# MLP down projections by rows: activations stationary, weights moving, and the last norm by rows

## What is computed

```python
D_MODEL, D_FF, SEQ = 1024, 4096, 512
...
h = _rmsnorm(x, mlp_norm_g)          # x: [512, 1024]
u = jnp.square(jax.nn.relu(h @ w_up))   # [512, 4096]
x = x + u @ w_down
return _rmsnorm(x, final_norm_g)
```

## Time and profile before

| what | value |
|---|---|
| median of 3 runs | 1023.85 us (1023.57 to 1024.23) |
| the profiled execution | 1023.27 us |
| its span, first to last instruction | 1021.5 us |
| PE busy | 1012.0 us (99%) |
| DVE, ACT, POOL busy | 52%, 42%, 57% |
| DMA share of 16 engines (queue q1) | 29.2% |
| granted TensorE clock, mean | 0.999 |

### The profile page before, as it was taken

One profiled execution on the slowest core, in us unless ns is written; L12 is line 12 of the kernel. 1 busy time (PEld: TensorE's weight loads), 2 busy tenths in 40 slices (PEclk: granted clock), 3 DMA queues, 4 the chain that ended last, 5 costly groups with the idle time before them and its releaser, 6 DMA issues.

```text
span 1021.5 us, 12838 instructions
## 1 busy us (share of the span) xinstructions
PE 1012.0 (99%) x5063; PEld 857.5 (84%) x5063; DVE 527.4 (52%) x895; ACT 425.0 (42%) x687; POOL 582.3 (57%) x724
## 2 busy tenths in 40 slices
PE   9999999999999999999999999999999999999997
PEld 8888888888888888888899977888888888888887
DVE  5781356775366843445679997846123113212323
ACT  4653455556534524443346685533223212222332
POOL 4555556556565774565557877447545545545441
PEclk9999999999999999999999999999999999999999
DMA  6322222122352125323123123222322322322312
GB/s 230 128 83 85 85 81 83 42 83 83 115 174 83 48 76 188 124 83 118 52 79 124 43 83 114 92 84 83 123 84 83 123 83 83 124 83 83 121 45 83
DMA packets 93788, 98.63 MB, mean 97 GB/s; under 512 B 3314, under 2 KB 88848, under 8 KB 93728
## 3 DMA queue, kind: packets, MB, share of 16 engines
q1 hardware_dynamic: 93728, 97.81, 29.2%
HBM read 95.71 MB, written 2.10 MB: 96 GB/s over the span
## 4 chain that ended last, share of the span: by engine, by line
PE 92%; DVE 6%; ACT 1%; issue 1%; DVEq 0%
PE ps L383 82%; PE ps L771 1%; PE ps L1803 1%; PE ps L271 1%; PE ps L803 1%; PE ps L724 1%; PE ps L722 1%; PE ps L428 1%; PE ps L503 1%; DVE ps L1286 0%; DVE tmp L1352 0%; DVE Fm L1243 0%; PE ps L932 0%; DVE Hl L1324 0%; DVE Al L1711 0%
## 5 line engine op out<-in xcount | busy, mean ns | idle before, releaser
L296 POOL TENSOR_TENSOR wlo<-raw,whi 128x256 fp32r<-128x256 f32 x664 | 515.5, 808 | 339.0 <-ACT whi L291 339.0
L383 PE MATMUL ps<-Hh,whi 128*128 128x512 f32 x816 | 321.0, 393 | 1.6 <-DVE Hl L1324 1.2
L383 PE MATMUL ps<-Hl,whi 128*128 128x512 f32 x816 | 318.0, 390 | 0.0
L291 ACT ACTIVATE whi<-raw 128x1024 fp32r<-128x1024 f32 x166 | 175.2, 1055 | 158.9 <-PE ps L383 151.0
L383 PE MATMUL ps<-Hh,wlo 128*128 128x512 f32 x816 | 205.1, 389 | 0.3 <-POOL wlo L296 0.3
L383 PE MATMUL ps<-Ah,whi 128*128 128x512 f32 (+1 forms) x576 | 196.4, 364 | 0.2 <-DVE Al L1711 0.2
L383 PE MATMUL ps<-Al,whi 128*128 128x512 f32 (+1 forms) x576 | 194.7, 361 | 0.0
L383 PEld LDWEIGHTS ps<-Hh,whi 128*128 128x128 f32 x816 | 153.3, 188 | 33.8 <-DVE Hl L1324 1.9
L383 PEld LDWEIGHTS ps<-Hh,wlo 128*128 128x128 f32 x816 | 153.1, 188 | 32.5 <-POOL wlo L296 0.7
L383 PEld LDWEIGHTS ps<-Hl,whi 128*128 128x128 f32 x816 | 153.3, 188 | 30.8
L383 PE MATMUL ps<-Ah,wlo 128*128 128x512 f32 (+1 forms) x576 | 124.5, 360 | 0.0
(11 more groups left out here) (324 smaller groups left out, 1013.7 us busy)
## 6 DMA issues: line engine op xcount, KB each, us to landing
raw<-in_w_in SPq DMA_DIRECT2D x33, 1024.0 KB, 5.1
raw<-in_w_up SPq DMA_DIRECT2D x16, 1024.0 KB, 5.4
raw<-in_w_down SPq DMA_DIRECT2D x16, 1024.0 KB, 5.1
raw<-in_w_att_out SPq DMA_DIRECT2D x4, 1024.0 KB, 5.1
raw<-in_w_sg_out SPq DMA_DIRECT2D x4, 1024.0 KB, 5.2
raw<-in_w_o SPq DMA_DIRECT2D x4, 1024.0 KB, 5.1
raw<-in_w_in SPq DMA_DIRECT2D x6, 512.0 KB, 3.7
Fm<-in_x SPq DMA_DIRECT2D x2, 1024.0 KB, 6.7
```

Of the source, the lines that this page charges most:

```text
L291: eh = A(lambda e, s=s, src=src, kk=kk: e.activation(wtile(whi, s, kk), src, ACT.Copy), raw_ev[b], used)
L296: el = G(lambda e, s=s, src=src, kk=kk, cut=cut: e.tensor_tensor(wtile(wlo, s, kk)[:, *cut], src[:, *cut], f(wtile(whi, s, kk))[:, *cut], ...
L383: return e.matmul(ps[:, bk, 0:c1 - c0], wt, x[:, k, c0:c1], start=st, stop=sp)
```

## The change

The down weights come in half-megabyte blocks of one tile: 256 rows by 512 columns. A down pass takes one half of the output columns (512) for all 512 tokens: four banks, one per 128 tokens; the stationary operand is a 128x128 block of activations, the moving one 512 columns of weights, and each weight tile serves four banks. The sums are added on DVE to a residual held by rows, `OT`, which is made once: `residual_turns`, a background generator during part 0, transposes the residual's eight tiles through banks 7 and 6. The up products of parts 1 to 3 rotate over all eight banks. The gains of the last norm are loaded once, copied to all partitions. The last 512 columns of part 3 are not a pass: their four weight tiles are kept whole in `Ah`/`Al` (free after the last up product), and each block of 128 tokens runs its 24 matmuls, then its add, square with a running sum (ACT, `accum_out`), factor, scaling and store, while the next block multiplies. The square sums by matmul, the transposes and the halves at the end are gone.

```diff
         for i in range(4):
             cols("w_up_2", 0, 1024 * i, 4)
-            cols("w_down_2", 1024 * i, 0, 4)
...
+            for h in range(2):
+                for k in range(4):
+                    cols("w_down_2", 1024 * i + 256 * k, 512 * h, 1, 2, 1)
+        n_kept = len(tiles) - 4
+
+
+        kept = [tuple(a[:, 1024 * i:1024 * i + 1024].rearrange("p (k n) -> p k n", k=2) for a in (Ah, Al))
+                for i in range(4)]
...
+                kk = blocks[b][3]
...
-                used = w_used[j - NW] if j >= NW else None
...
+                if j < n_kept:
+                    th, tl = wtile(whi, j % NW, kk), wtile(wlo, j % NW, kk)
+                    used = w_used[j - NW] if j >= NW else None
+                else:
+                    (th, tl), used = kept[j - n_kept], got["up"]
+                eh = A(lambda e, th=th, src=src: e.activation(th, src, ACT.Copy), raw_ev[b], used)
...
-                    el = G(lambda e, s=s, src=src, kk=kk, cut=cut: e.tensor_tensor(
-                        wtile(wlo, s, kk)[:, *cut], src[:, *cut], f(wtile(whi, s, kk))[:, *cut], ALU.subtract),
-                        eh, signal=(part == 3))
+                    el = G(lambda e, th=th, tl=tl, src=src, cut=cut: e.tensor_tensor(
+                        tl[:, *cut], src[:, *cut], f(th)[:, *cut], ALU.subtract), eh, signal=(part == 3))
...
-        OT = F1.rearrange("p k n -> p (k n)").rearrange("p (t c) -> p t c", t=4)
-        ot_ev = []
+        OT, Z = (F.rearrange("p k n -> p (k n)").rearrange("p (t c) -> p t c", t=4) for F in (F1, F2))
+        ot_ev = [[], []]
...
-        def turn(n, ev):
...
+        def residual_turns():
+            yield
+            yield
+            for i, n in enumerate(late_k):
+                bk = 7 - i % 2
+                for t_ in range(4):
+                    et = T(lambda e, t_=t_, n=n, bk=bk: e.transpose(
+                        ps[:, bk, 128 * t_:128 * t_ + 128], F3[:, n, 128 * t_:128 * t_ + 128], ident[:]),
+                           hm_ev[n], bank_free[bk], signal=(t_ == 3))
+                bank_free[bk] = A(lambda e, n=n, bk=bk: e.activation(
+                    OT[:, :, 128 * n:128 * n + 128], ps[:, bk, :].rearrange("p (t c) -> p t c", t=4), ACT.Copy),
+                    et, hm_ev[3])
+                ot_ev[n // 4].append(bank_free[bk])
+                if i < 7:
+                    yield
+
+        def four_banks():
+            bks = sorted(range(8), key=lambda bk: bank_age[bk])[:4]
+            taken(*bks)
+            return bks
+
+        def down_mm(bk, t_, k, w, x, start, stop, signal):
+            return T(lambda e: e.matmul(ps[:, bk, :], x[:, k, 128 * t_:128 * t_ + 128], w, start=start, stop=stop),
+                     signal=signal)
+
+        def down_pass(ahead=(3, 3, 3, 3)):
+
+            bks = four_banks()
+            q.wait("pe", *[bank_free[bk] for bk in bks])
...
+                j = at[0]
+                at[0] += 1
+                feed(j + ahead[i])
+                q.wait("pe", hi_ev[j])
+                wh, wl = wtile(whi, j % NW, 2), wtile(wlo, j % NW, 2)
+                ks = (2 * i, 2 * i + 1)
+                order = [(k, wh, x) for k in ks for x in (Hh, Hl)] + [(k, wl, Hh) for k in ks]
+                for n, (k, w, x) in enumerate(order):
+                    q.wait("pe", *acts[k], lo_ev[j] if w is wl else None)
+                    evs = [down_mm(bks[t_], t_, k, w[:, k % 2], x, i == 0 and n == 0, i == 3 and n == 5, n == 5)
+                           for t_ in range(4)]
+                w_used.append(evs[3])
+                tick()
+            return bks, evs
+
+        def down_add(h, t_, bk, em):
+            y = OT[:, t_, 512 * h:512 * h + 512]
+            e_ot[t_, h] = bank_free[bk] = V(lambda e: e.tensor_tensor(y, ps[:, bk, :], y, ALU.add), em, *ot_ev[h],
+                                            e_ot.get((t_, h)))
...
+        e_ot = {}
         bgs.append(mlp_factors())
+        bgs.append(residual_turns())
         for part in range(4):
             acts = []
-            nb = 6 if part < 3 else 4
             waiting = []
             for n in range(8):
...
+                waiting.append(single(A8h, A8l, u3ev, late_k, nb=8 if part else 6))
 
...
+            got["up"] = w_used[-1]
+            if part == 0:
+                while bgs:
+                    finish(bgs[0])
+                gl = P[:, 0:1024]
+                e_gl = q.dma("sp", gl, t["final_norm_g_2"].rearrange("(a n) -> a n", a=1).broadcast_to([128, 1024]),
+                             dsem("d_gl"), got["ss"])
+            for h in range(2 if part < 3 else 1):
+                bks, evs = down_pass((3, 3, 3, 3) if part < 3 else (3, 5, 6, 5))
+                for t_ in range(4):
+                    down_add(h, t_, bks[t_], evs[t_])
+            e_down = evs[3]
+
+
+
...
+        R4, ssq, v4 = sm[:, 180:184], sm[:, 146:154], sm[:, 154:162]
         d_out = dsem("d_out")
...
+        def squares(h, t_):
+            y, z = (a[:, t_, 512 * h:512 * h + 512] for a in (OT, Z))
+            c = 2 * t_ + h
+            ea = A(lambda e: e.activation(F4[:, c], y, ACT.Square,
+                                          accum_out=ssq[:, c:c + 1]), e_ot[t_, h], got["ss"], hm_ev[3])
+            ez = V(lambda e: e.tensor_tensor(z, y, gl[:, 512 * h:512 * h + 512], ALU.mult), e_ot[t_, h], e_gl)
+            return ea, ez
+
+        first_half = {}
+        for t_ in range(4):
+            ea, ez = squares(0, t_)
+            e0 = V(lambda e, t_=t_: e.tensor_scalar(v4[:, t_:t_ + 1], ssq[:, 2 * t_:2 * t_ + 1], 1.0 / D, EPS, ALU.mult,
+                                                    ALU.add), ea)
+            first_half[t_] = (ez, e0)
+        js = range(at[0], at[0] + 4)
+        at[0] += 4
+        bks = four_banks()
+        for t_ in range(4):
+            order = [(k, 0, x) for k in range(8) for x in (Hh, Hl)] + [(k, 1, Hh) for k in range(8)]
+            q.wait("pe", bank_free[bks[t_]])
+            for n, (k, part, x) in enumerate(order):
+                q.wait("pe", (lo_ev if part else hi_ev)[js[k // 2]])
+                em = down_mm(bks[t_], t_, k, kept[k // 2][part][:, k % 2], x, n == 0, n == 23, n == 23)
+            down_add(1, t_, bks[t_], em)
+            ea, ez1 = squares(1, t_)
+            ez0, e0 = first_half[t_]
+            r = R4[:, t_:t_ + 1]
+            e1 = V(lambda e, t_=t_: e.scalar_tensor_tensor(
+                v4[:, 4 + t_:5 + t_], ssq[:, 2 * t_ + 1:2 * t_ + 2], 1.0 / D, v4[:, t_:t_ + 1], ALU.mult, ALU.add), ea, e0)
+            e2 = V(lambda e, t_=t_: e.reciprocal(v4[:, 4 + t_:5 + t_], v4[:, 4 + t_:5 + t_]), e1)
+            er = A(lambda e, t_=t_, r=r: e.activation(r, v4[:, 4 + t_:5 + t_], ACT.Sqrt), e2)
+            ev = V(lambda e, t_=t_, r=r: e.tensor_scalar(Z[:, t_, 0:512], Z[:, t_, 0:512], r, None, ALU.mult), er, ez0)
+            q.dma("sp", out_v[:, t_, 0:512], Z[:, t_, 0:512], d_out, ev)
+            ev = A(lambda e, t_=t_, r=r: e.activation(Z[:, t_, 512:1024], Z[:, t_, 512:1024], ACT.Copy, scale=r), er, ez1)
+            e_out = q.dma("sp", out_v[:, t_, 512:1024], Z[:, t_, 512:1024], d_out, ev)
+        w_used.extend([em] * 4)
```

More of the change, by code:

```diff
@@ L286, in feed @@
                     load_block()
-                s, kk = j % NW, blocks[b][3]
+                kk = blocks[b][3]
                 n = 1024 // kk
                 src = raw_block(b)[:, :, i * n:i * n + n]
-                used = w_used[j - NW] if j >= NW else None
-                eh = A(lambda e, s=s, src=src, kk=kk: e.activation(wtile(whi, s, kk), src, ACT.Copy), raw_ev[b], used)
+                if j < n_kept:
[4 more added lines that the diff above has]
+                eh = A(lambda e, th=th, src=src: e.activation(th, src, ACT.Copy), raw_ev[b], used)
                 hi_ev.append(eh)
@@ L1738, in mlp_factors @@
             got["R3"] = yield from spread(RB, R3, 6, factors(R3))
-        def turn(n, ev):
-            s, fr = new_tmp()
-            eg = V(lambda e: e.tensor_scalar(tmp[:, s, 0:512], F3[:, n], g_l[:, n:n + 1], None, ALU.mult), ev, fr)
+        def residual_turns():
             yield
-            tb = 4 + n % 2
-            for i in range(4):
[L1747 to L1754, removed]
+            yield
[11 more added lines that the diff above has]
+                    yield
@@ L1756, in build @@
+        def down_add(h, t_, bk, em):
[3 more added lines that the diff above has]
+        e_ot = {}
         bgs.append(mlp_factors())
+        bgs.append(residual_turns())
         for part in range(4):
             acts = []
-            nb = 6 if part < 3 else 4
             waiting = []
             for n in range(8):
-                waiting.append(single(A8h, A8l, u3ev, late_k, nb=nb))
+                waiting.append(single(A8h, A8l, u3ev, late_k, nb=8 if part else 6))
@@ L1773, in build @@
                     acts.append([ev])
[L1774 to L1782, removed]
@@ L1783, in build @@
-            e_down = em
-        R4 = sm[:, 180:184]
-        d_out = dsem("d_out")
```

(2 more changed lines are left out.)

## The result

The changed kernel takes 1026.27 us (median of 11 runs, 1024.21 to 1026.83) against 1023.85 us (median of 11). The ratio is 1.002, 95% interval [1.0011, 1.0029]: slower by 2.4 us by the medians. That is clear of zero and lies about at the 0.2% (2.05 us) up to which the prediction speaks of no change. The profiled execution took 1026.6 us for a span of 1024.8.

The account below looks back on a forecast made before the run. TensorE, busy 99% of the span, was taken as the bound; -0.60 - 4.23 + 3.92 + 2.86 - 1.0 = +0.95 us on the median 1023.85 gave 1024.8 us, range 1022.2 to 1028.5.

Parts of the forecast that it names:

- Down products, +0: Down passes: matmuls going to a different bank each time keep their pace of 0.2267 us, adding 0.
- Rivals 2 and 4: Down matmuls, alternating banks: pitch falls, 1014.5 us, chance 0.06; or rises 5 ns or more, 1028.6 or worse, chance 0.05.
- What leaves part 3 and the halves, -4.83: Part 3: transposes and square sums leave, -4.23 us; four half products become whole ones, -0.6 us.
- Transposes +3.92 and their waits +2.86: Part 0: eight transpose groups at 0.49 us, +3.92; TensorE's waits at first group, second group and end, +2.86.
- The stall is 1.86: End of part 0: first down pass waits for copies of the last two residual groups, 1.86 us.
- Feeding by half megabytes, +0: Down weight loads: one-tile buffers are copied, split and reloaded in time, so no wait, 0.
- The last 512 columns, +0: Last block of part 3: four kept tiles ready in time, spare 2.7 us for high part, 2.1 for low.
- Rival 1: Last block: kept tiles come late, TensorE stalls 3.1 and 2.2 us, 1030.1 us; chance 0.27 including smaller delays and longer waits.
- The tail, -1.0: After the last matmul: second store issued at about T+3.2 instead of T+4.2, saving 1.0 us.
- Rival 3: Part 0: waits mostly covered, without the 2.86 us the time is 1021.9 us; chance 0.10.

Follow-up runs that it names:

- the filled wait: Changed kernel with six useless matmuls run in the wait before the first down pass: 1024.49 us, ratio 1.0006.
- the fastest version: Changed kernel, first down pass on the up products' banks, residual groups one product later on bank 7, last three behind tiles of that pass: 1021.56 us.

## Why the prediction was right and where it fell short

The forecast was 1024.8 us with a range to 1028.5 and no measurable change as the likeliest; measured were 1026.27 and a change about at that bound. That the range held is in part luck: its upper end was there for the kept tiles coming late, which did not happen, while the clock, which did, had no term; and the tail, taken 0.7 us too dear, gave back part of what the clock cost. Point by point:

- **Down products, +0: right.** In the changed kernel's chain 192 down matmuls of part 3 take 43.53 us, and in the timeline of its first pass groups of four start 0.90 us apart, although each of the four goes to another bank:

```profile
975.53 43.53 PE ps L1773 x192
...
719.69 1.07 PE L1773 MATMUL ps<-whi,Hh 128*128 128x512 f32 x4
720.59 1.07 PE L1773 MATMUL ps<-whi,Hl 128*128 128x512 f32 x4
```

  0.2267 us each, as in the earlier trace rows. Rivals 2 and 4, the pitch cases, are out.
- **What leaves part 3 and the halves, -4.83: right**, once the clock is taken out: -2.95 measured less 1.78 of the clock is -4.73. The parts 1 to 3 have no wait of TensorE, as the text said.
- **Transposes +3.92 and their waits +2.86: right**, +6.9 together. The three places are where the text put them, 0.26, 0.78 and 1.36 + 0.25 in the list. The timelines at the end of part 0, changed kernel (L523 scaling, L1815 square, L550 split, L1760 residual copies):

```profile
709.38 0.69 DVE L523 TENSOR_TENSOR tmp<-ps,Rb 128x512 f32<-128x512 f32 x1 [2.65 <-PE ps L392]
710.11 0.69 DVE L1815 SCALAR_TENSOR_TENSOR tmp<-tmp 128x512 f32<-128x512 f32 x1
...
710.83 0.63 ACT L550 ACTIVATE Hh<-tmp 128x512 fp32r<-128x512 f32 x1 [0.42 <-DVE tmp L1815]
711.37 1.07 ACT L1760 ACTIVATE Fm<-ps 128x512 f32<-128x512 f32 x2
...
712.48 1.34 PE L1773 MATMUL ps<-whi,Hh 128*128 128x512 f32 x4 [1.36 <-ACT Fm L1760]
```

  With S = 709.18 the scaling came at S+0.20, the split at S+1.65, the pass at S+3.30 (3.33 in the text).
- **The step that failed** is the end of "Their waits": "The stall is 1.86". The stretch up to the pass was sized well (3.33 us, measured 3.30), but priced at its own length alone. The granted clock was read as full and the sum carried it as a constant; with the wait it fell, and the lower clock cost 1.78 us more (the filled wait). 1024.8 + 1.8 would have been 1026.6.
  The Trainium skill (TensorE: Matmul & The Clock Gate, Part 1) says that the throttled state is the default and that activity releases it. The traces agree as far as they go: 1.00 where TensorE works without a break, 0.50 behind the stretch of 3.30 us with twelve transposes and two waits.
- **Feeding by half megabytes, +0: right.** No wait of a pass for a copy or a split. The page of the changed kernel has the 32 loads at 3.4 us to landing:

```profile
raw<-in_w_down SPq DMA_DIRECT2D x32, 512.0 KB, 3.4
```

- **The last 512 columns, +0: right.** Kept tile 3 in the timelines of ACT and POOL, changed kernel:

```profile
995.90 1.06 ACT L301 ACTIVATE Ah<-raw 128x1024 fp32r<-128x1024 f32 x1 [2.52 <-DMA raw<-in_w_down]
...
997.04 3.29 POOL L306 TENSOR_TENSOR Al<-raw,Ah 128x256 fp32r<-128x256 f32 x4 [0.76 <-ACT Ah L301]
```

  The last block starts four times 5.44 ahead of T = 1019.06, at 997.3, and wants the low part 4.99 later, at 1002.3; it was there at 1000.3. The spare was 2.0 us where the text had 2.1. Rival 1 did not happen, but when forced it cost more than its price.
- **The tail, -1.0: too small,** -1.7. The order was right; two terms were off. The chain of the changed kernel (L1841 is the square with its read, L1871 the scaling), and the stores (durations, first and last issue):

```profile
1019.81 0.73 ACT Fm L1841 x2
...
1021.19 0.72 ACT Fm L1871
```

```profile
L54 SPq DMA_DIRECT2D out<-Fm x8: 332/396/433, 1005.4 to 1022.1; - x8
```

  The square with its read is 0.73 and not 0.80, since the read starts before the square's end; the last store is issued at T+3.04 instead of T+3.2. And the end follows it by 2.7 us instead of the 3.2 of before. Stores now land 2.0 to 2.3 us after their issue, before 2.1 to 3.3, when the last four were issued within 1.3 us; that fewer at a time is the reason wasn't tried.
- **Rival 3**, waits covered, was not what this kernel does, but it is what the fastest version does: 1021.56 against the 1021.9 worked out for it.

With both corrections the sum stands at +0.95 + 1.8 - 0.7 = +2.05; measured +2.4, and +2.2 between the traces where they differ by the change.

## What to carry to other kernels

Where TensorE is busy all the time, price a long new wait twice: its length, and the matmuls behind it at half the clock, and look for the second in the windows' clock column, since the busy share reads 100% through it. Count the transposes next to a wait with it: the wait of 1.36 us behind twelve of them was followed by the fall, one of 1.63 behind ordinary matmuls was not. When background work shares a rotating resource with the main line (banks here), start it so that no main step takes the resource that the background used last; choosing four other banks was worth 3.7 us, more than the whole change gains without its waits (2.3). Finish the last group block by block and not all at once: that order was worth 7 us.

## What the runs showed of the hardware that I had not expected

- A wait of TensorE of 1.36 us, behind twelve transposes and a wait of 0.25, was followed by 3.4 us at 1.2 GHz, beginning 0.9 us after TensorE had gone on. With 0.25 to 0.3 us as the longest wait in the same place the clock stayed full, and so it did behind a wait of 1.63 without transposes.
- Not every run seems to pay alike: the 11 runs of the changed kernel spread over 2.6 us, those with the wait removed over 0.8, with it filled over 0.9, and the kernel before over 0.9. The changed kernel's three fastest runs (1024.21 to 1025.23 us) are also the only ones with a mean granted clock of 0.999 or 1.000, the others have 0.998; 3.4 us at half clock lower the mean by 0.0017. That speaks for the clock, but weakly: among the runs with all waits away the mean varies from 0.998 to 1.000 too, and the time does not follow it.
- In this kernel a matmul has a fixed cost of about 13 ns at either width (0.2267 us for 512 columns, 0.1196 for 256; twice the second less the first), and it is the same whether neighbours share a bank or not (the earlier trace rows and the rows of the first pass above).
- GpSimd's splits took 2.82 us in one kept tile and 3.29 in the last, where DVE's multiplications with both inputs in SBUF ran beside the end of them (from 999.05 on), 0.47 more. The second of these multiplications took 1.16 us instead of 0.69, also 0.47 more: both engines were slowed, and neither was shut out for the other's whole length.
